# Moving rotary angles, a short convolution and index logits, and a deeper ring in one feed-forward stage, in a float32 two-block transformer kernel on Trainium2

## What is computed

```python
def dwconv3(x, w, b):                      # over tokens
    xp = jnp.pad(x, ((0, 0), (1, 1), (0, 0)))
    return xp[:, :-2] * w[0] + xp[:, 1:-1] * w[1] + xp[:, 2:] * w[2] + b

def conv_ffn(h, w_up, conv_w, conv_b, w_down):        # first block, x and ctx
    ug = dwconv3(h @ w_up, conv_w, conv_b)            # 1024 -> 2 x 2816
    u, g = jnp.split(ug, 2, axis=-1)
    return (jax.nn.silu(g) * u) @ w_down

def short_conv_mixer(gate_b, gate_c, h, conv_w):      # second block, 256 columns, 3 taps
    u = gate_c * h
    u_pad = jnp.pad(u, ((0, 0), (CONV_K - 1, 0), (0, 0)))
    y = conv_w[0] * u_pad[:, 0:S]
    for j in range(1, CONV_K):
        y = y + conv_w[j] * u_pad[:, j:j + S]
    return gate_b * y

def hybrid_mixer(x, positions, w_in, conv_w, rel_bias, w_out):
    (cb, cc, ch, dq, dk, dv, iq, ik, iw, cq, ck, cv) = jnp.split(x @ w_in, offs, axis=-1)
    y_conv = short_conv_mixer(cb, cc, ch, conv_w)
    # dq, dk, iq, ik = partial_rope(..., positions): angles from integer positions
    # dsa_attention: per query score = sum_h iw_h * relu(iq_h . ik) over 8 index heads;
    #   the 128 best keys are kept, then softmax attention over them
    # chunk_band_attention: causal by chunks of 64, with a relative bias table
    return concat([y_conv, y_dsa, y_chk]) @ w_out
```

## Time and profile before

| | |
|---|---|
| three runs, median | 3885.47 us (3875.17 to 3890.61) |
| profiled execution, its own time | 3878.89 us |
| its span | 3877.1 us, 49749 instructions, mean granted TensorE clock 0.954 |
| TensorE / VectorE / ScalarE / GpSimd busy | 93% / 47% / 42% / 42% |
| chain that ended last, by engine | PE 81%, DVE 11%, ACT 4%, issue 3%, POOL 1%, DMA 1% |
| DMA | 355.56 MB, mean 92 GB/s |
| context feed-forward stage | about 1066 to 1281 us |
| last feed-forward stage of the first block | about 1770 to 2131 us |
| mixer's projection, layer 0 and 1 | about 2134 to 2310, and 3001 to 3167 us |
| attention behind it | to about 2383, and 3240 us |

### The profile page before, as it was taken

One profiled execution on the slowest core, in us unless ns is written; L12 is line 12 of the kernel. 1 busy time (PEld: TensorE's weight loads), 2 busy tenths in 40 slices (PEclk: granted clock), 3 DMA queues, 4 the chain that ended last, 5 costly groups with the idle time before them and its releaser, 6 DMA issues.

```text
span 3877.1 us, 49749 instructions
## 1 busy us (share of the span) xinstructions
PE 3590.7 (93%) x19478; PEld 2836.0 (73%) x19478; DVE 1837.1 (47%) x2966; ACT 1620.6 (42%) x2660; POOL 1611.6 (42%) x978
## 2 busy tenths in 40 slices
PE   6999877999999999979999889999999989989998
PEld 4766555788789776557888666977887767877886
DVE  6754644442275664744322586353114586252114
ACT  5446645442354437633432235434322334444222
POOL 2544431444467644313444331524444422524442
PEclk8999987999999999989999989999999999999998
DMA  8433221333345622213333321412333311413331
GB/s 249 115 98 99 88 71 37 94 98 93 93 144 166 153 80 88 88 33 92 95 96 93 77 65 33 131 55 76 98 94 80 85 49 44 131 44 93 97 94 60
DMA packets 642465, 355.56 MB, mean 92 GB/s; under 512 B 70469, under 2 KB 614841, under 8 KB 642233
## 3 DMA queue, kind: packets, MB, share of 16 engines
q1 hardware_dynamic: 630451, 339.67, 30.9%
q10 hardware_dynamic: 11782, 12.71, 1.0%
HBM read 346.28 MB, written 6.05 MB: 91 GB/s over the span
## 4 chain that ended last, share of the span: by engine, by line
PE 81%; DVE 11%; ACT 4%; issue 3%; POOL 1%; DMA 1%; DVEq 0%; ACTq 0%
PE psum L808 63%; PE psum L964 5%; PE psum L988 3%; PE psum L1006 2%; ACT work L1357 1%; DVE neg_max L1779 1%; PE psum L884 1%; POOL w_lo L788 1%; DVE sel_mask L2121 1%; PE psum L1035 1%; DVE top L2120 1%; PE psum L915 1%; PE psum L847 1%; PE psum L934 1%; ACT w_hi L1231 1%
## 5 line engine op out<-in xcount | busy, mean ns | idle before, releaser
L788 POOL TENSOR_TENSOR w_lo<-w_raw,w_hi 128x1024 fp32r<-128x1024 f32 (+2 forms) x956 | 1588.3, 1678 | 2168.9 <-ACT w_hi L1231 2168.6
L808 PE MATMUL psum<-h_hi,w_hi 128*128 128x512 f32 (+1 forms) x3024 | 1159.6, 383 | 85.0 <-DVEq L1623 29.5
L808 PE MATMUL psum<-h_lo,w_hi 128*128 128x512 f32 (+1 forms) x3024 | 1124.3, 372 | 0.0
L808 PE MATMUL psum<-h_hi,w_lo 128*128 128x512 f32 (+1 forms) x3024 | 1123.4, 372 | 0.0
L1231 ACT ACTIVATE w_hi<-w_raw 128x1024 fp32r<-128x1024 f32 (+1 forms) x626 | 655.1, 1047 | 713.1 <-PE psum L808 633.4
L808 PEld LDWEIGHTS psum<-h_hi,w_hi 128*128 128x128 f32 x3024 | 580.0, 192 | 233.5 <-issue 60.7
L808 PEld LDWEIGHTS psum<-h_lo,w_hi 128*128 128x128 f32 x3024 | 582.4, 193 | 99.1 <-issue 8.9
L808 PEld LDWEIGHTS psum<-h_hi,w_lo 128*128 128x128 f32 x3024 | 581.2, 192 | 97.0
L808 PE MATMUL psum<-hid_hi,w_hi 128*128 128x512 f32 (+1 forms) x1040 | 392.4, 377 | 3.9 <-POOL w_lo L788 3.9
L808 PE MATMUL psum<-hid_lo,w_hi 128*128 128x512 f32 (+1 forms) x1040 | 391.2, 376 | 0.0
L808 PE MATMUL psum<-hid_hi,w_lo 128*128 128x512 f32 (+1 forms) x1040 | 391.1, 376 | 0.0
(11 more groups left out here) (211 smaller groups left out, 3906.5 us busy)
## 6 DMA issues: line engine op xcount, KB each, us to landing
w_raw<-in_w_up_dram SPq DMA_DIRECT2D x132, 512.0 KB, 3.8
w_raw<-in_w_ff_dram SPq DMA_DIRECT2D x128, 512.0 KB, 3.9
w_raw<-in_w_in_dram SPq DMA_DIRECT2D x92, 512.0 KB, 3.8
w_raw<-in_w_ada_dram SPq DMA_DIRECT2D x80, 512.0 KB, 3.9
w_raw<-in_w_down_dram SPq DMA_DIRECT2D x48, 512.0 KB, 3.9
w_raw<-in_w_mkv_dram SPq DMA_DIRECT2D x32, 512.0 KB, 4.0
w_raw<-in_w_down_dram SPq DMA_DIRECT2D x24, 384.0 KB, 3.3
w_ada_first<-in_w_ada_dram SPq DMA_DIRECT2D x4, 2048.0 KB, 19.6
```

Of the source, the lines that this page charges most:

```text
L788: m = nc.gpsimd.tensor_tensor(WL[:, c % NSPLIT, k:k + step, :], RAW[:, c % NRAW, k:k + step, :], WH[:, c % NSPLIT, k:k + step, :].bitcast( ...
L808: m = pe.matmul(out_ap, lhs(a, k), rhs(b, k), start=(k == 0 and n == 0), stop=(k == nk - 1 and n == 2))
```

## The change

1. The four rotary tables are computed in the last feed-forward stage of the first block: one table's VectorE instructions before `residual` at every second down tile of group 0, their Sines at down tiles 2 to 5 of group 1. Positions are loaded at that stage's start. The buffers are others, since `pos_int` moves into `work`.
2. `beside` gets a half: it is called before a tile (0) and in its middle (1; on TensorE before the fifth of its eight slices). Index logits start at step 4: four in steps 4 and 5 each, two before and two in the middle of the tile, then two a step. Rounds start at step 7: 1, 1, 1, 3, 3, 3, 4 for query tile 3, then four a step; the last are at step 21.
3. The relative bias's flips go to steps 1 to 3 (VectorE's part to 2 to 4) and into banks 4 and 5. The first logits additionally wait for pair 2, the transposes of tile 3 for pair 1. The copy of the causal mask moves from step 19 to 2.
4. The short convolution leaves VectorE for GpSimd, behind `w_lo` of the output projection's second chunk: seven instructions for each of two tiles. ScalarE's and VectorE's split of its result moves from before attention to its steps 15 to 17.
5. In the context stage `mid_u` and `mid_g` hold six tiles of 256 columns, and GpSimd makes `w_lo` in two operations of 512 columns where the chunk has eight slices.

```diff
-INDEX_FIRST, CONV_STEP = 5, 17
-def index_logits(step):
-    return [n for n in (2 * (step - INDEX_FIRST), 2 * (step - INDEX_FIRST) + 1) if 0 <= n < len(INDEX_STEPS)]
+INDEX_FIRST = 4
+ROUNDS = {3: (1, 1, 1, 3, 3, 3, 4), 2: (4, 4, 4, 4), 1: (4, 4, 4, 4)}
+ROUND_STEPS = [(t, sum(ROUNDS[t][:i]), n) for t in (3, 2, 1) for i, n in enumerate(ROUNDS[t])]
+def index_logits(step, half):
+    pair = 2 * (step - INDEX_FIRST) + half if step < INDEX_FIRST + 2 else step - INDEX_FIRST + 2 if half == 0 else -1
+    return [n for n in (2 * pair, 2 * pair + 1) if 0 <= n < len(INDEX_STEPS)]
 def index_rounds(step):
-    n = step - INDEX_FIRST - 4
-    return (3 - n // 4, 4 * (n % 4), 4) if 0 <= n < 12 else None
+    n = step - INDEX_FIRST - 3
+    return ROUND_STEPS[n] if 0 <= n < len(ROUND_STEPS) else None
...
+        def mids(T):
+            return 3 * SEQ // T
+        def mid(M, q, T):
+            return M[:, :, :].rearrange("p r c -> p (r c)").rearrange("p (q t) -> p q t", t=T)[:, q % mids(T), :]
+        CONV_AT = 15
...
+            def short_conv(l):
+                for m in range(2):
+                    cb, cc, ch = (QK2[:, 13 + 2 * i + m, :] for i in range(3))
+                    tap_of = QK2[:, 4, :]
+                    for i in range(3):
+                        pool.wait_ge(*at("raw_copied", (("mix_in", l), 8 + 2 * i + m)))
+                    own("cv_step", (l, m, "u"), nc.gpsimd.tensor_tensor(cc, cc, ch, ALU.mult))
+                    own("cv_step", (l, m, 2), nc.gpsimd.tensor_scalar(ch, cc, prm("conv_w_2", l * 6 + 4 + m), None, ALU.mult))
+                    pool.wait_ge(*at("idx_relu", (l, len(INDEX_STEPS) - 1)))
+                    for back, tap in ((1, 1), (2, 0)):
+                        own("cv_step", (l, m, tap, "scaled"), nc.gpsimd.tensor_scalar(
+                            tap_of, cc, prm("conv_w_2", l * 6 + 2 * tap + m), None, ALU.mult))
+                        own("cv_step", (l, m, tap), nc.gpsimd.tensor_tensor(ch[:, back:SEQ], ch[:, back:SEQ],
+                                                                          tap_of[:, 0:SEQ - back], ALU.add))
+                    own("cv_step", (l, m, "y"), nc.gpsimd.tensor_tensor(ch, ch, cb, ALU.mult))
...
+                    if c == IDS["mix_out", l][AHEAD]:
+                        short_conv(l)
...
-                step = 2 if name in ("w_in", "w_in_2") else nk
+                step = 2 if name in ("w_in", "w_in_2") else 4 if c in IDS["ffn", "c", 0] and nk == KT else nk
...
                 for k in range(nk):
+                    if k == 4 and amid is not None:
+                        amid()
...
                         if S[0] == "mix_in" and j > INDEX_FIRST:
                             pe.wait_ge(*at("idx_relu", (S[1], len(INDEX_STEPS) - 1)))
+                        elif S[0] == "mix_in":
+                            pe.wait_ge(*at("bias_step", ("rel", S[1], 1)))
...
-                    if CONV_STEP - 4 <= step < CONV_STEP - 1:
-                        pair = step - CONV_STEP + 4
+                    if 1 <= step < 4 and half == 0:
+                        pair = step - 1
                         if pair == 0:
                             pe.wait_ge(*at("bias2_in", (l, 5)))
-                            pe.wait_ge(*at("rope_step", (("mix_in", l), 7, "sin")))
...
                         if n == 0:
                             pe.wait_ge(*at("rope_step", (("mix_in", l), 2, "sum")))
                             pe.wait_ge(*at("v_copied", (("mix_in", l), 3)))
+                            pe.wait_ge(*at("bias_step", ("rel", l, 2)))
...
+                    if S[0] == "att2" and CONV_AT <= i < CONV_AT + 2:
+                        m = i - CONV_AT
+                        act.wait_ge(*at("cv_step", (S[1], m, "y")))
+                        nc.scalar.activation(HH[:, m, :], QK2[:, 17 + m, :], ACT.Copy).then_inc(*mark("cv_hi", (S[1], m)))
...
-                    if q >= 3:
-                        act.wait_ge(*at("hid_lo", (S, q - 3)))
+                    if q >= mids(T):
+                        act.wait_ge(*at("hid_lo", (S, q - mids(T))))
...
                     if step[0] == "down":
+                        if S == ("ffn", "x", DEPTH - 1) and step[1] == 1 and 2 <= step[2] < 6:
+                            sine(step[2] - 2)
...
+                    if S[0] == "att2" and CONV_AT < i <= CONV_AT + 2:
+                        m = i - CONV_AT - 1
+                        dve.wait_ge(*at("cv_hi", (S[1], m)))
+                        lo("cv_lo", (S[1], m), HL[:, m, :], QK2[:, 17 + m, :], HH[:, m, :])
...
+                        if S == ("ffn", "x", DEPTH - 1) and g == 0 and k % 2:
+                            angle(k // 2)
                         residual(S, down, cs[n], PS[:, 4 + down % 4, 0:T], k, T, x, gate(k), ALPHA if g == 0 else 1.0,
```

More of the change, by code:

```diff
@@ L901, in ada_turn, with project @@
                 return m
-            def project(S, tiles, cs, T, rots, normed, beside=lambda i: None):
+            def project(S, tiles, cs, T, rots, normed, beside=lambda i, half: None):
                 n = len(tiles)
                 for i in range(n + 2):
-                    beside(i - 1)
+                    beside(i - 1, 0)
                     if i < n:
@@ L1261, in norm, with project @@
                         *mark("h_hi", (S, k)))
-            def project(S, tiles, cs, T, dst, off, beside=lambda i: None):
+            def project(S, tiles, cs, T, dst, off, beside=lambda i, half: None):
                 n = len(tiles)
                 for i in range(n + 1):
-                    beside(i - 1)
+                    beside(i - 1, 0)
                     if i < n:
                         split_ahead(cs[i])
+                        beside(i - 1, 1)
                         t = tiles[i]
@@ L1390, in attend, with sine @@
                             *mark("o_hi", (S, o)))
+            def sine(i):
+                act.wait_ge(*at("trig_step", (i, "max")))
+                nc.scalar.activation(ROPE2[:, i, :], ROPE2[:, i, :], ACT.Sin).then_inc(*mark("trig_act", i))
             def ffn(S, cs, T, l, groups, parts, x, rms=None, ln=None, first=None):
@@ L1553, in _, with beside @@
                     act.dma_start(TBK[:, h, :], bass.AP(REL_PAD.tensor, (l * 6 + h) * 384, [[1, P], [1, 256]])).then_inc(*mark("bias2_in", (l, h), 16))
-                def sines(tables):
-                    for i in tables:
-                        act.wait_ge(*at("trig_step", (l, i, "max")))
-                        nc.scalar.activation(ROPE2[:, i, :], ROPE2[:, i, :], ACT.Sin).then_inc(*mark("trig_act", (l, i)))
-                def beside(step):
-                    if step == 2 and l == 0:
-                        sines((0, 1))
-                    for n in index_logits(step):
+                def beside(step, half):
+                    for n in index_logits(step, half):
                         t = INDEX_STEPS[n][0]
@@ L1568, in beside @@
                                              ACT.Relu).then_inc(*mark("idx_relu", (l, n)))
-                if l == 0:
-                    sines((2, 3))
                 project(("mix_in", l), mixer_tiles(), IDS["mix_in", l], SEQ, QK2, 0, beside)
                 stage_end()
-                for m in range(2):
-                    nc.scalar.activation(HH[:, m, :], QK2[:, 17 + m, :], ACT.Copy).then_inc(*mark("cv_hi", (l, m)))
                 attend(attention_plan_2(l))
@@ L1670, in norm, with project @@
                                                            *mark("h_lo", (S, j)))
-            def project(S, tiles, cs, T, dst, off, tables, v_dst, beside=lambda i: None):
+            def project(S, tiles, cs, T, dst, off, tables, v_dst, beside=lambda i, half: None):
                 n = len(tiles)
@@ L2095, in beside @@
-                def beside(step):
-                    if step == 2 and l == 0:
-                        angles((0, 1))
-                    if step == INDEX_FIRST:
+                def beside(step, half):
+                    if 2 <= step < 5 and half == 0:
+                        pair = step - 2
+                        ps = PS[:, 4 + pair % 2, :].rearrange("p (h c) -> p h c", h=2)
+                        dve.wait_ge(*at("rel_flipped", (l, pair)))
+                        nc.vector.tensor_copy(TBK[:, 2 * pair:2 * pair + 2, 0:P], ps[:, :, 0:P]).then_inc(
+                            *mark("bias_step", ("rel_low", l, pair)))
+                        nc.vector.tensor_tensor(TBK[:, 2 * pair:2 * pair + 2, P:2 * P], ps[:, :, P:2 * P],
+                                                CAUSAL.unsqueeze(1).broadcast_to([P, 2, P]), ALU.add).then_inc(
+                                                    *mark("bias_step", ("rel", l, pair)))
+                    if step == INDEX_FIRST and half == 0:
@@ L2115, in beside @@
                             own("idx_step", (l, t, "causal"), nc.vector.tensor_tensor(last, last, CAUSAL, ALU.add))
-                    if index_rounds(step) is not None:
```

(4 more changed lines are left out.)

119 lines of the change are left out of this document (49 added, 70 removed).

## The result

| | before | after |
|---|---|---|
| median of the first comparison | 3885.38 us (3875.17 to 3890.61) | 3846.32 us (3844.76 to 3848.49) |
| ratio, 95% interval | | 0.9903, 0.9882 to 0.9924 |
| profiled execution, span | 3877.1 us | 3844.0 us |
| TensorE busy, mean granted clock | 93%, 0.954 | 93%, 0.955 |

The changed kernel was run again beside later experiments: 3849.42 us, ratio 0.9919 (0.9904 to 0.9934). So it is 0.8 to 1% faster: the medians lie 39.1 us apart in the first comparison and 27.7 in the second, where the kernel before had a median of 3877.14. The forecast was 3849, 36.7 under the kernel before.

The account below looks back on a forecast made before the run. TensorE, busy 93% with split products, was taken as the bound, so only its idle or slow time could be won. 11.7 + 16.2 + 6.4 - 10.6 + 1.0 + 12.0 = 36.7 us off 3885.5 gave 3849, range 3833 to 3866.

Parts of the forecast that it names:

- 1, rotary angles: Layer 0's mixer projection: moving the tables to the last feed-forward stage removes waits and a slow tile, 11.7 us won.
- the cover: Last feed-forward stage's group-0 down tiles: 23.4 us left beside w_lo, so 20.4 us of angles fit without delaying TensorE.
- 2, index order and bias: Mixers' projections: earlier index work and bias remove the bias-step wait, 16.2 us, and the end's arrears, 6.4, over two layers.
- the second part: Projection's end: rounds done a tile earlier and no convolution there remove the last transposes' wait, 3.2 us a layer, 6.4.
- term 4: Convolution on GpSimd, hidden with some 35 us to spare; head of attention 1.2 us sooner, 0.7 lost mid-attention a layer: +1.0.
- 3, the new wait: First logits, directly behind tile 2's rotation: 3.6 us idle plus 1.7 of slow clock, 5.3 lost a layer, 10.6 together.
- the slower rival: Convolution's scalar operations on GpSimd very slow, delaying attention; from 10.6 us each the whole gain is lost; chance 0.03.
- 5, the context stage: Context feed-forward: six middle tiles and halved w_lo bring VectorE's pair under TensorE's, 12 us won, bounds 0 and 18.
- halves don't help: Context stage: GpSimd starts its second half at once, VectorE stays out for both, term 5 gives nothing: 3861; chance 0.14.
- GpSimd becomes the bound: Context stage: VectorE operations also hold GpSimd up, a pair costs 7.7 us instead of 6.9: 3879; chance 0.05.

Follow-up runs that it names:

- ring of three: Changed kernel with three middle tiles in the context stage instead of six: 3846.2 us with w_lo in halves, 3857.5 us with w_lo whole.
- quarters: Changed kernel with the context stage's w_lo in four pieces of 256 columns instead of two of 512: 3854.1 us, ratio 0.9920.
- the early exponential: Changed kernel plus a one-column exponential on ScalarE at the projection's end: 3842.2 us; with logits later 3827.8, with whole w_lo too 3834.1.

## Why the prediction was right, and where it was not

**The time.** 3849 was forecast, and 3846.3 and 3849.4 were measured. The stages that the change touches were to give -36.7, and gave -37.6. Some of this is luck: the context stage gave 4.7 us more than its term, and the two projections and the attentions behind them gave 3.9 less than theirs.

**1, rotary angles, 11.7: right in kind, though the cover was mis-sized.** Taking the move back costs 9.7, and the stage that took them in did not grow. But the cover was counted as 23.4 us against 20.4 of angles, with the residuals' 6.2 left out, and with nothing for the time that an angle instruction spends waiting for w_lo. VectorE was in fact busy for 40.3 of 44.7 us. The groups beside those down tiles:

```profile
L1909 DVE TENSOR_SCALAR rope<-rope 128x512 f32<-128x512 f32 x4 | 10.5, 2619 | 0.1
L1904 DVE TENSOR_SCALAR work<-work 128x512 f32<-128x512 f32 x4 | 8.0, 1988 | 0.1
```

One of these operations takes 0.43 us when left alone, and two of each table took 2.5 to 2.7. A table takes 9.1 to 9.3 us, not 5.0, and the 4.4 us left would not have held a fifth. That TensorE saw nothing fits the forecast's point that it wants `residual` only four tiles later; no run tests it.

**2, index order and bias, 16.2 + 6.4: the sizes hold, the reason of the second part fails.** Layer 0's and layer 1's stretches are within 0.4 and 1.6 us of the sums. No run undid the order of the flips alone, so the 16.2 rest on that agreement and on the waits that are gone. The step that failed is "with the rounds done one tile earlier": by the schedule the last rounds are at step 21, where they had been at 20. They are later, and it is the convolution's leaving that frees the end. The kernel with the convolution back shows it: from the start of the last tile to the first scores 13.1 us, against 10.8 before and 7.9 after. So the move to GpSimd, whose part in the end had been left to both, is worth 5 us a layer and carries the whole 3.2; under term 4 the forecast had given it nothing of its own. The sizes hold in part by luck too: in layer 1 the tile behind the flips was only 1.1 us over in the kernel before (6.78 us), not 1.6. And with the 9.7 measured for the angles and 6.3 a layer for the new wait put in, what is left for this term is some 13.9 us in layer 0 and 10.7 in layer 1, an estimate from the stage lengths, where 11.3 each had been summed.

**3, the new wait, 5.3 a layer: right in kind, a little small.** The gap is 3.46 us (3.6 forecast), and the slow clock behind it costs (2.07 - 1.06) + (4.81 - 2.95) = 2.9 us where 1.7 was taken; the bound was 3.1. The granted clock was 0.56 over those 6.8 us, so nearly all of it at 1.2 GHz. A step's delay of the logits returns 6.1 and 6.0.

**4, the head of attention, 1.0: lost.** That the table load "now starts 1.15 us sooner" was wrong. As I read the two timelines, the copy in front of the load had carried the wait for the stage's end (the load ran at 2311.24, before the first maximum at 2312.40); without it the exponential itself carries that wait and the one for the first maximum, and the load stands behind a wait for the maximum. So 0.35 us was won instead of 1.15, and the first exponential comes at 4.04 instead of 4.39 us after TensorE's drain. With the 0.7 a layer taken for the split in the middle, that makes a loss of 0.7 in two layers; 0.9 was measured (0.2 and 0.6, rounded). No run shows the 0.7 by itself. GpSimd's operations ended with 33 us to spare (35 forecast), and the slower rival, which needed over 10.6 us for an operation with a scalar, fell at 1.57. The Trainium skill, GPSIMD Engine Reference, engine selection, calls one-input work roughly line rate, from which 1.3 us had been worked out as a bound; the measured 1.57 is above it, and above the two-input 1.27 to 1.29 of the same shape.

**5, the context stage, 12: 16.7 and 15.3 were measured, within the bounds of 0 and 18, but the cause was shared out wrongly.** The forecast let the halves bring VectorE's pair under TensorE's and the ring only pass it on. Alone the halves are worth 11.8 us, but the ring alone is worth 16 to 19, and the halves add nothing to it. The rival "halves don't help" was right of this kernel and wrong in its reason and its price. Its reason was that VectorE stays out for both halves, and with the ring of three it stays out for one (1.51 us); its price left the ring nothing. "GpSimd becomes the bound" is not seen with halves, where it is busy for 65 of 75 us and a meeting costs it 0.18 us (1.47 instead of 1.29, ring of three), and it is seen with quarters.

On what the meeting of two engines costs: a `hid_lo` of 0.42 us takes 2.62 us when it meets whole w_lo, 1.51 with halves and 0.96 with quarters, each time 0.2 more than GpSimd's operation (2.4, 1.3, 0.77). With a shared bandwidth, cutting would have changed nothing. The Trainium skill, SBUF — State Buffer, two separate sides, has it as a lock held for a whole instruction; this comparison agrees.

## What to carry to other kernels

When two engines slow each other inside their instructions, look first at what fixes their phase: a deeper ring let them miss each other, and cutting the operations then had nothing left to give. Work moved onto an engine beside another's long operations is to be costed with one short operation stretched to the length of the other's for each of those that it meets (here two of the nine of a table, 4 us more), not at its undisturbed time. And when a wait is moved ahead of an engine that had a tile to cover it, start the dependent work a tile later: the wait cost twice, once as a gap and once as a slow clock.

## What the hardware showed that was not expected

- **A busy VectorE may be a waiting one.** Timelines of VectorE, then GpSimd, beside the first angle of the changed kernel:

```profile
1937.63 0.48 DVE L1900 TENSOR_SCALAR rstd<-acc,const_sb 128x512 f32<-128x512 f32 x1
1938.15 2.51 DVE L1902 TENSOR_SCALAR work<-rstd 128x512 f32<-128x512 f32 x1
1940.70 0.43 DVE L1904 TENSOR_SCALAR work<-work 128x512 f32<-128x512 f32 x1
```
```profile
1937.71 2.67 POOL L826 TENSOR_TENSOR w_lo<-w_raw,w_hi 128x1024 fp32r<-128x1024 f32 x1 [0.99 <-ACT w_hi L1274]
```

  VectorE's first operation was under way when GpSimd's began, and GpSimd's took 2.67 us where 2.40 is usual; VectorE's second ended at 1940.66, 0.28 us behind GpSimd's end at 1940.38. It reads as if each had waited for the other's whole instruction. Nothing in a share of busy time tells this: the same 22 products and 22 `hid_lo` of the context stage kept VectorE busy for 25.1 + 46.6 us before and for 10.3 + 10.3 after, 51 us less. (Its busy total over the program fell by 57, from 1837.1 to 1780.4; the convolution's twenty instructions took 19.6 away, and the angles grew by some 17.)
- **GpSimd is slower with one tensor than with two**: 1.57 us for a 128x512 multiplication by a scalar, 1.27 to 1.29 for one of two tensors.
- **The load of an activation table stands where the first exponential's waits let it**, here between the wait for the maximum and the exponential, which put 1.28 us on the chain.
- **A gain at the head of attention did not reach its end.** Stretches at half clock lay at other steps in each kernel and gave or took 1 to 4 us: layer 1's attention took 78.1 us twice with the early exponential, 73.5 to 74.5 in most others. In the trace the granted clock was at half for 20.4 us of it in those two kernels, and for 10.2 in the changed one and in the two without the early exponential. What sets where they fall stays open.
